# The gains of the input norm spread by TensorE, the square root's table loaded first, parameters on two queues, and another order of loads in a prologue

## What is computed

```python
def _rmsnorm(x, g):
    y = xf * lax.rsqrt(jnp.mean(xf * xf, axis=-1, keepdims=True) + EPS)
    return (y * g.astype(jnp.float32)).astype(x.dtype)
...
h = _rmsnorm(x, g)                       # g = norm_gain, 2048 numbers
proj = h @ w_in                          # u | z_ssm | q | k | v | z_att | f_pre
y_ssm, hT_re, hT_im = _s5_scan(u, log_dt, a_re, a_im, b_re, b_im, c_re, c_im, d, h0_re, h0_im)
...
y = jnp.concatenate([y_ssm, y_att], axis=-1)
x = x + (y @ w_out).astype(x.dtype)
```

## Time and profile before

| | |
|---|---|
| median of 3 runs | 1975.07 us (1973.59 to 1975.46) |
| profiled execution | 1973.29 us, span 1971.7 us |
| busy: PE, DVE, ACT, POOL | 98%, 51%, 33%, 21% of the span |
| prologue, until the first piece of the main loop | to 90.2 us of the span |
| instructions | 30996 |

### The profile page before, as it was taken

How to read it: one execution, slowest core, us unless ns; L and a number is a source line. 1 busy time by engine, 2 the same in 40 slices (tenths; PEclk the granted TensorE clock), 3 DMA queues, 4 the chain that set the end, 5 groups by cost and what they waited for, 6 DMA issues and landing times.

```text
span 1971.7 us, 30996 instructions
## 1 busy us (share of the span) xinstructions
PE 1934.9 (98%) x10736; PEld 1756.9 (89%) x10736; DVE 1013.2 (51%) x1993; ACT 654.9 (33%) x1266; POOL 408.9 (21%) x706
## 2 busy tenths in 40 slices
PE   5999999999999999999999999999999999999999
PEld 4899999999989999999999999999998988888887
DVE  7865666555454553645546355463576662222221
ACT  6423333333342343333433343334354441111110
POOL 5865454555210010010100101001010021010100
PEclk8999999999999999999999999999999999999999
DMA  9344343344322122121211213112175452222221
GB/s 228 104 109 113 110 110 104 107 116 125 98 55 63 36 59 61 32 86 35 73 45 35 86 32 84 37 37 82 32 237 176 142 200 92 93 94 91 96 87 49
DMA packets 194129, 180.03 MB, mean 91 GB/s; under 512 B 32178, under 2 KB 165388, under 8 KB 192852
## 3 DMA queue, kind: packets, MB, share of 16 engines
q1 hardware_dynamic: 176832, 127.97, 23.5%
q0 software_dynamic: 11712, 40.12, 6.1%
q10 hardware_dynamic: 5524, 11.14, 1.7%
HBM read 133.24 MB, written 45.93 MB: 91 GB/s over the span
## 4 chain that ended last, share of the span: by engine, by line
PE 85%; DVE 9%; issue 3%; ACT 2%; DMA 1%; SPq 0%; DVEq 0%; POOL 0%; ACTq 0%; POOLq 0%
PE GB L212 39%; PE GB L223 8%; PE TB L2148 4%; PE TB L2149 4%; PE TB L2150 4%; PE TB L2035 3%; PE TB L2056 3%; PE GB L2148 2%; PE GB L2150 2%; PE GB L2149 2%; PE GB L226 2%; PE GB L222 2%; PE TB L2077 2%; DVE M L832 1%; PE TB L1180 1%
## 5 line engine op out<-in xcount | busy, mean ns | idle before, releaser
L212 PE MATMUL GB<-X,whi 128*128 128x416 f32 x3264 | 908.9, 359 | 0.2 <-DVE wlo L201 0.2
L212 PEld LDWEIGHTS GB<-X,whi 128*128 128x128 f32 x3264 | 598.2, 188 | 30.9 <-issue 11.9
L212 PE MATMUL GB<-X,wlo 128*128 128x416 f32 x1632 | 572.4, 351 | 0.0
L201 DVE TENSOR_TENSOR wlo<-wraw,whi 128x256 fp32r<-128x256 f32 x412 | 199.3, 485 | 446.8 <-ACT whi L197 442.3
L197 ACT CAST whi<-wraw 128x256 fp32r<-128x256 f32 x412 | 166.3, 405 | 605.8 <-PE GB L223 595.8
L223 PE MATMUL GB<-X,whi 128*128 128x512 f32 x816 | 323.6, 397 | 1.2 <-DVE UP L789 0.3
L212 PEld LDWEIGHTS GB<-X,wlo 128*128 128x128 f32 x1632 | 306.3, 188 | 2.3
L223 PEld LDWEIGHTS GB<-X,whi 128*128 128x128 f32 x816 | 153.3, 188 | 6.0 <-DVE UP L789 3.4
L1455 POOL DMA_DIRECT2D ya_s<-ZR x7 | 4.1, 584 | 721.5 <-DVE ZR L1839 721.5
L1886 DVE RECIPROCAL SQ<-SQ 128x136 f32<-128x136 f32 x128 | 127.6, 997 | 1.1
L1635 ACT ACTIVATE PR<-PR,nmx 128x128 f32<-128x128 f32 (+8 forms) x72 | 53.4, 741 | 185.0 <-DVE nmx L1857 173.4
(11 more groups left out here) (432 smaller groups left out, 2830.1 us busy)
## 6 DMA issues: line engine op xcount, KB each, us to landing
wraw<-in_w_in SPq DMA_DIRECT2D x380, 128.0 KB, 2.2
OLF<-in_w_out SPq DMA_DIRECT2D x48, 256.0 KB, 2.7
XO<-in_x_prompt POOLq DMA_DIRECT2D x32, 256.0 KB, 4.2
out_y_prompt<-XO POOLq DMA_DIRECT2D x24, 256.0 KB, 2.8
xt<-in_x_prompt SPq DMA_DIRECT2D x5, 1024.0 KB, 5.4
NCB<-nc_s POOLq DMA_DIRECT2D x8, 608.0 KB, 4.5
us_s<-UP SPq DMA_DIRECT2D x8, 548.0 KB, 3.2
U<-us_s SPq DMA_DIRECT2D x64, 68.5 KB, 3.1
```

Source lines behind the costliest of these rows:

```text
L201: V.tensor_tensor(wlo[:, s % SPL], wraw[:, s % RAW], whi[:, s % SPL].bitcast(f32), ALU.subtract).then_inc(self.lo, 1)
L212: ins = T.matmul(main(b), w[:, s % SPL, kk], self.x[:, half, k + kk, c:c + n], start=first and kk == 0 and i == 0, stop=last and kk == PIE ...
```

## The change

It edits only the prologue.

1. **Gains.** The two broadcasts go. One row of 8 KB is loaded (`gain_row`). PE multiplies it with a row of 64 ones, in four banks of `TB` by two halves of 64 output partitions, and DVE copies the result into `gain[0]` and `gain[1]`. This comes first on PE and first on DVE.
2. **Tile 1** is asked for directly behind that row.
3. **Table.** ACT runs a root on a constant before it waits for tile 0.
4. **Parameters.** Six of the eleven loads (`vin`) are issued by POOL behind its identity and mask and counted by a semaphore of their own, `ld_vec`; DVE's copy of the step sizes waits for the other five alone.
5. **Order on DVE.** `x_scale` is split into `x_norm` and `x_scale`; for tile 0 the copies of the transposed parameters now stand between the two.
6. **C and B** are asked for two tiles later.

```diff
+            gain_row = pkf[0:1, 8 * P:8 * P + D_MODEL]
+            ones_row = pkf[0:1, 24 * P:24 * P + 64]
...
                 sp.dma_start(x_all(0), x_prompt[0, 0:P].rearrange("p (k c) -> p k c", k=KT)).then_inc(ld_x[0], 16)
-                for i in range(2):
-                    sp.dma_start(gain[i], norm_gain[0:1, :].to_broadcast([P, D_MODEL]).rearrange("p (k h c) -> p h k c", k=KT, h=2)[:, i]
-                                 ).then_inc(ld_gain, 16)
+                sp.dma_start(gain_row, norm_gain).then_inc(ld_gain, 16)
...
-                    if m in (4, 5):
-                        for i in range(8 * (m - 4), 8 * (m - 3)):
+                    if m in (6, 7):
+                        for i in range(8 * (m - 6), 8 * (m - 5)):
                             load_c(i)
-                    if m == 6:
+                    if m == 8:
                         for i in range(4):
                             load_b(i)
...
                 act.wait_ge(ident_done, 2)
                 o = Order(act, "act_order")
+                o.then(S.activation(tabs[:], epsc[:], ACT.Sqrt))
...
-                def x_scale(m):
+                def x_norm(m):
...
-                    if m == 0:
-                        dve.wait_ge(ld_gain, 32)
+
+                def x_scale(m):
+                    n = rows[m]
                     for b in range(2):
                         x = x_all(m)[:, :, 64 * b:64 * (b + 1)]
-                        ins = V.scalar_tensor_tensor(x, x, y, gain[b][0:n], ALU.mult, ALU.mult)
+                        ins = V.scalar_tensor_tensor(x, x, ssq[0:n, m, 5:6], gain[b][0:n], ALU.mult, ALU.mult)
                     ins.then_inc(xs_done, 1)
...
-                dve.wait_ge(ld_par, 16 * 11)
+                dve.wait_ge(gain_mm, 1)
+                for i in range(2):
+                    ins = V.tensor_copy(gain[i], TB[:, 0:D_MODEL].rearrange("p (k h c) -> p k h c", k=KT, h=2)[:, :, i])
+                o.then(ins)
+                dve.wait_ge(ld_par, 16 * 5)
                 V.tensor_copy(pin[:, 2].rearrange("r (g p) -> r g p", g=2),
                               ldt.unsqueeze(2).to_broadcast([32, 2, NP])).then_inc(dt_bc, 1)
                 dve.wait_ge(ident_done, 2)
                 V.tensor_reduce(delta[:], ident[:].rearrange("p (g c) -> p c g", c=GC), AX.X, ALU.add)
-                x_scale(0)
+                x_norm(0)
                 dve.wait_ge(par_t, 1)
                 V.tensor_copy(vec[:], GB[:, 0:34]).then_inc(par_ev, 1)
                 V.tensor_copy(prm[:].rearrange("p a b -> p (a b)"), GB[:, 64:224]).then_inc(par_ev, 1)
+                x_scale(0)
                 for m in range(TT):
                     if m + 1 < TT:
+                        x_norm(m + 1)
                         x_scale(m + 1)
                     x_rest(m)
...
+                G.memset(ones_row, 1.0)
                 G.memset(epsc[:], EPS)
...
+                pool.dma_start(vin[0:8], ssm_d[0].rearrange("(r g) c -> r (g c)", g=8)).then_inc(ld_vec, 16)
+                pool.dma_start(vin[8:16], row128(b_glu)).then_inc(ld_vec, 16)
+                pool.dma_start(vin[16:24], row128(ssm_out_norm)).then_inc(ld_vec, 16)
+                pool.dma_start(vin[24:32], row128(att_out_norm)).then_inc(ld_vec, 16)
+                pool.dma_start(vin[32:33], q_norm_gain).then_inc(ld_vec, 16)
+                pool.dma_start(vin[33:34], k_norm_gain).then_inc(ld_vec, 16)
...
                 pe.wait_ge(ident_done, 2)
-                pe.wait_ge(ld_par, 16 * 11)
+                pe.wait_ge(ld_gain, 16)
+                for b in range(4):
+                    for r in range(2):
+                        ins = T.matmul(TB[64 * r:64 * r + 64, 512 * b:512 * (b + 1)], ones_row, gain_row[:, 512 * b:512 * (b + 1)],
+                                       start=True, stop=True)
+                ins.then_inc(gain_mm, 1)
+                pe.wait_ge(ld_par, 16 * 5)
+                pe.wait_ge(ld_vec, 16 * 6)
                 pe.wait_ge(dt_bc, 1)
```

More of the change, by code:

```diff
@@ L310, in build_kernel @@
             sem(n) for n in ("ld_gain", "ld_u", "ld_par", "ld_b", "ld_c", "st_pk", "ld_wf"))
+        gain_mm, ld_vec = sem("gain_mm"), sem("ld_vec")
         ident_done, par_t, par_ev, dt_bc = sem("ident_done"), sem("par_t"), sem("par_ev"), sem("dt_bc")
@@ L493, in scalar @@
             def scalar(act):
-                def row128(a):
-                    return a.rearrange("o (r p) -> (o r) p", p=P)
                 act.dma_start(ldt, ssm_log_dt[0].rearrange("(r g) -> r g", g=2)).then_inc(ld_par, 16)
@@ L901, in gpsimd, with row128 @@
                                 pattern=[[-1, P]], channel_multiplier=1).then_inc(ident_done, 2)
+                def row128(a):
+                    return a.rearrange("o (r p) -> (o r) p", p=P)
+                pool.dma_start(vin[0:8], ssm_d[0].rearrange("(r g) c -> r (g c)", g=8)).then_inc(ld_vec, 16)
[4 more added lines that the diff above has]
+                pool.dma_start(vin[33:34], k_norm_gain).then_inc(ld_vec, 16)
                 def exp_poly(out, x, n):
@@ L1247, in attention @@
             e = {n: sem("att_" + n) for n in names}
-            spent = [(ld_gain, 32), (ld_u, 16), (ld_par, 16 * 11), (ld_b, 16 * 4), (ld_c, 16 * 16), (ld_wf, 16), (ld_x[TT - 1], 16), (gate_out, 48),
+            spent = [(ld_gain, 16), (ld_u, 16), (ld_par, 16 * 5), (ld_b, 16 * 4), (ld_c, 16 * 16), (ld_wf, 16), (ld_x[TT - 1], 16), (gate_out, 48),
                      (ident_done, 2), (par_t, 1), (par_ev, 2), (dt_bc, 1), (sq_done, TT), (xs_done, TT), (x_t, 4 * TT),
```

## The result

| | before | changed |
|---|---|---|
| median, range (17 runs each) | 1975.07 us (1972.82 to 1978.66) | 1979.03 us (1975.97 to 1982.25) |
| ratio to before | | 1.0022 [1.0015, 1.0028] |
| profiled execution, its span | 1973.29, 1971.7 us | 1975.97, 1974.4 us |

The change makes the kernel slower, by 0.22% by the ratio and by 4.0 us (0.20%) by the medians: 0.7 above the forecast of 1978.3, inside its range, and just beyond what I had called no change.

What follows compares the result with a forecast made beforehand. PE is busy 98% of the span, so only the prologue's DVE chain, before PE runs unbroken from 50 us, could move the time. Tile 1's +2.0 and a 1.15 us gap gave +3.2 on 1975.07: 1978.3 us, range 1974.0 to 1982.0.

Steps and rivals of the forecast that it cites:

- step (c): Gains' products on PE: row usable not much before 6.2 us, products take 6.0 us, ending at G = 12.2.
- the clock's gain r: Continuous PE work at half speed before the clock rises, 3.65 to 5.7 us; products last r + (7.3 - r)/2.
- (a): SP's queue without broadcasts: tile 1 lands at 9.0 instead of 14.6 us, its square and root done by 11.5.
- (b): ACT's table loaded during the wait for tile 0, no second load: tile 0's root ready at 8.6, not 11.16 us.
- (d): DVE first copies gains from PSUM, 2.5 us; tile 0 scaled at G + 4.35 = 16.55, tile 1 2.0 us late.
- (e): Second DVE wait, before tile 2, for ACT's square behind tile 0's casts: gap 1.15 us, tile 2 scaled at 26.85.
- S: Shift of DVE's chain in the prologue, taken as the whole kernel's change in time: +3.2 us, or G - 9.0.
- (f): Six parameter loads on POOL's queue, 0.81 us each, ending near 7.5, landing about 12, needed at 14.7: no cost.
- (g): Later C and B loads: waits for tile 6 (ACT 1.92, DVE 1.01 us) go, but PE is full: no gain.
- halves don't overlap: Rival: each half of the gains' products waits for the other, G about 15.5, +6.5 us, 1981.6 us; 12%.
- Early row, early clock: Rival: row lands near 3.5 us and products run at full clock, 3.65 us; 1973.3 to 1975.9 us; 20%.
- ACT's gains: Rival: DVE not held by the products, tile 1's early root starts its chain near 12.5, -4.5 us, 1970.6; 3%.

Runs made afterwards that it cites:

- e9: Changed kernel with 40 unread transposes of the identity on PE ahead of the wait for the row of gains; 1980.71 us, single execution.
- e10: Changed kernel with 22 unread float32 products of the identity, 128 rows summed over, ahead of the gains' products; 1980.43 us, single execution.
- e11: Changed kernel with 22 unread float32 products of 128 columns, one row summed over, ahead of the gains' products; 1983.61 us, single execution.
- e4: Changed kernel with tile 0's norm ahead of DVE's copies of the gains, and parameter copies behind tile 0's scaling; 1978.81 us, single execution.
- e5: Changed kernel with ACT squaring tile 2 before its casts of tile 0; 1980.29 us, single execution.
- e7: Changed kernel with the loads of C and B put back where they were before; 1978.47 us, single execution.
- e3: Changed kernel with four gain products into 128 output partitions instead of eight into 64; 1981.96 us, single execution.
- e8: Changed kernel with the row of gains asked for first on ACT's queue instead of behind tile 0 on SP's; 1978.51 us, single execution.
- b2: Changed kernel with the row first on ACT's queue, tile 2 squared early, DVE copying gains bank by bank, small steps between; 1973.37 us, ratio 0.999 to before.
- e1: Changed kernel with the gains loaded again by two broadcast DMAs, all other edits kept; 1974.79 us, ratio 1.0002 to before.

## Why the prediction was right, and what it mis-sized

The forecast was the mechanism's own case, +3.2 us; the landmarks say +4.1 to +4.2, the medians +4.0. The 0.9 comes from one term of step (c): **the clock's gain r**. I had let continuous work raise the clock after 3.65 to 5.7 us, so that the products would take 6.0 us. They took 7.10, every one at half speed (I had priced that at 7.3), and ended at G = 6.39 + 7.10 = 13.49, not 12.2: 1.10 of the difference is their length, 0.19 the row's later start. Nor did r scatter: the products took 7.09 us in each of the eight profiled executions that made them once and had no rise of the clock ahead of them. e9 and e10 show that both the price at full clock (3.65) and the length of work before a rise (about 5.5 us of transposes; by the same reckoning about 4.4 of full-height products, with 0.222 and 0.112 us per instruction) lay in my bounds; e11 shows that they do not hold for one-row work. All the work that I had read the clock from was of full height. The point "if it starts at half speed, when does it rise?" was taken over from them without asking whether a single row counts as work.

The other steps held, and those on the path were a little under their price. (a) Tile 1 landed at 9.9, predicted 9.0; its root ended at 12.2, not 11.5, and neither was waited for. (b) The table load went as said; tile 0's root was there at 8.8 (8.6). (d) From G to the scaling of tile 0 it took 4.18 (4.35), and tile 1 followed 3.35 later (3.4). (e) The second wait came, 0.73 + 0.24 = 0.97 us (1.15), and tile 2 was scaled 10.18 after tile 0 (10.3). Together S = G + 4.18 + 10.18 - 23.66 = 4.19: 1.29 more from G, 0.29 less from (d) and (e). e4 and e5 confirm both as real costs on the path: 1.5 us at tile 5 for the first, 1.07 at tile 2 and 0.57 at tile 5 for the second. (f) POOL's six issues took 0.51 to 0.71 each, not 0.81, and ended at 6.3; the last load landed 5.1 us after its issue, near 10.9 (12), and nobody waited. (g) Nothing was gained, as e7 shows. The waits for tile 6 went, but by e7 they would have gone with B in its old place too, the prologue being later.

Of the rivals, *halves don't overlap* is out by e3. If each half waited for the other, the eight divided products, whose instructions are listed as long as the undivided ones, would have taken twice the four undivided; they took as long (7.09 and 7.16). *Early row, early clock* was two conditions: e8 and b2 show that the row can be early if it is put on another queue, so "not held up by tile 0" was false for its place in SP's queue; the early clock came only in e9 and e10, behind work of full height. With the products at full clock G would have been 10.0 and S near +0.7 by the measured steps: the half speed, 3.45 us, is most of the loss. *ACT's gains* are real and needed G below 5; b2 gets at them differently, by letting DVE take bank after bank.

The number is better than the reasoning behind r. G = 13.49 lies outside the 11.2 to 12.9 to which I had given 50%, and the first sign that I had named, DVE's first copy at 11 to 13 us, was missed at 13.51. What came is the next case, the same mechanism with S of +4 to +5.5, for "a later row, a longer r or a further gap", to which I had given 15%; and r was not just longer, it had no end within these products. The steps behind G, 0.29 us cheaper than priced, took part of that back. With 29% for slower by over 0.2% and 67% for no change, I had leaned to the wrong side of a line that the medians passed by 0.1 us.

## What to carry to other kernels

A transfer of 1 MB can be replaced by products with a row of ones, but the price of such products is to be taken from TensorE at its cold speed: at the start of this kernel, one-row float32 products ran at half clock for as long as any run went on with them (16.8 us), and each bank should be handed on as it is made. A small load on which everything waits belongs at the head of a queue that has nothing large in it; here this alone was worth 2.6 us at tile 5. And before counting early loads as a gain, look for what the consumer waits for next: e1 had all of the change's edits to ACT, to the order on DVE and to the parameters' queues, and came out the same as before.

## What the hardware showed unexpectedly

- Products that sum over one row did not raise TensorE's clock in 7.1, 13.9 or 16.8 us of unbroken work; with 128 rows it rose after about 4.4 (products) and 5.5 us (transposes). The Trainium skill (TensorE: Matmul & The Clock Gate, "The HAM clock gate") says that the clock is set by how busy the engine has been lately. The trace agrees for full-height work only: PE is listed as busy throughout the leading work of e10 and e11 alike, and only the height told them apart.
- The granted clock read 1.00 in windows in which every instruction took its half-speed time (e11, 8 to 16 us), up to the first change in that column.
- Two float32 products of 64 output partitions took the time of one of 128 (7.09 and 7.16 us for all): for one-row products dividing gained nothing over undivided ones, and cost nothing.
- A row of 8 KB asked for directly behind 1 MB in the same queue was usable at 6.39, with the megabyte itself (6.46); first in the other queue it was usable at 3.79 in e8, and by 2.78 in b2, two single executions with the same order of loads up to there.
- In the main loop two executions with the same work can differ by several microseconds: the windows 520 to 560 and 1580 to 1620 had a granted clock of 1.00 and 1.00 in the changed kernel's, 1.00 and 0.96 in that of before, 0.91 and 0.91 in those of e3 and b2.
